# Stick-breaking attention: the norm of a head pair's second token half, in two parts in the sixth and eighth tile instead of whole in the fourth

## The chip, the cores and the metric

The kernel runs on one core of a Trainium2 chip. The metric is the device time of one execution in microseconds (us). Engines are named PE (TensorE, matmuls; PEld its weight loads), DVE (VectorE), ACT (ScalarE), POOL (GpSimd) and SP (SyncE, which starts the transfers). Each engine runs its own instruction stream in order, and the streams meet at semaphores.

## The reference, cut to what matters

The program is two transformer blocks over 1024 tokens of width 1024, in float32. The change lies in the attention of the second block. Eight heads of 64 channels are worked on; the weights of a head are

```
A[t,s] = sigmoid(z_ts) * prod_{s<j<t} (1 - sigmoid(z_tj)),  strictly causal, in log space
o_sb   = A v
y_sb   = rms_norm_2(o_sb, ones)            # over the 64 channels of each head
         * g_sb
mix    = concat(y_pool, y_sb) @ w_out
rms_norm_2(x, g) = x * rsqrt(mean(x*x) + 1e-6) * g
```

The change is in the `rms_norm_2` over each head.

## The kernel before, in words

**Layout.** Channels lie on the 128 partitions and tokens along a row, so a pair of heads fills the partitions. The four pairs are the rounds c = 0 to 3 of the loop at L2592. The 1024 queries are two halves of 512 (`H2`); a half and a block of 128 keys make a tile. `sb_pairs` (L103) lists the NP = 12 tiles p of a round: p = 0 to 3 for the first half (key blocks 3 to 0), p = 4 to 11 for the second (blocks 7 to 0). Each has both heads side by side; its width is 2x128, 2x256, 2x384 and 2x512 for the first four, the same for p = 4 to 7, then 2x512 to the end.

**A tile.** PE makes the scores (`z_pair`, L1160 and L1165). ACT makes log(1+exp(-|z|)) in three steps (`lse`, L1755, L1757, L1759). DVE adds max(z,0) (`softplus`, L2597) and splits the result into a high part (L2608) and a low part (L2610) (`split`). PE applies a triangular matrix to both (`tri_pair`, L1174, L1178) and sums them for the later tiles (`sums_pair`, L1190). DVE adds the sums of earlier tiles (`add_sums`, L2625; for the first tile of a half it clears them instead, L2618), ACT takes the exponent (`weights`, L1782) and copies the sums (`later_sums`), PE multiplies with the values (`pv_pair`, L1203).

**The order of one step p, by hand, on each engine.**
- PE: z(p+1), then at p = 4 and 6 of rounds 0 to 2 four transposes of the next round's values (`turn_v`, L1241), tri(p), sums(p), pv(p-1), then in rounds 0 to 2 `pieces(p)` (L1228): twelve matmuls of the next round's projections, four steps to a unit of weights. z(p+1) waits until add_sums(p-1) has freed its PSUM banks.
- ACT: lse(p+1), at p = 4 and 6 a copy of the turned values, weights(p), later_sums(p+1).
- DVE: split(p), at even p of rounds 0 to 2 `evac2` (L2570: one half unit of pieces, from PSUM, times the token scale), `head_mean` or `head_norm` where they are due, softplus(p+1), add_sums(p), and in round 3 at p = 3 to 9 `mix_lo(p-3)` (L2129), which waits for `mix_hi` of ACT. turn_v(0) at p = 4 waits for the evac2 of step 4, and that one for the last pieces of step 3.
- POOL: only the split of weight units (L628, L630; 128x1024 each). A unit's split starts when the matmuls of the unit before have ended, so at the end of pieces(3), pieces(7) and pieces(11).

**The norm.** Half m = 2c or 2c+1 of a round is copied out and squared by ACT (`out_half`) when its last tile is done, and the rest comes in the next round: PE takes the mean over each head (`head_mean`, L1254), DVE copies it into the tile `HM` (L2632) at p = 0 for the first half and p = 2 for the second, ACT makes a first guess of the inverse root (`head_guess`, L1797 and L1799, into `work_a`) at the end of the same step, and DVE refines and applies it (`head_norm`, four instructions on 128x512: L2639, L2641, L2643, L2645) at p = 1 and at p = 3, between split(p) and softplus(p+1). Round 0 has none of these. Round 3 has the first half of its own pair too, at p = 8 and 9; the last half comes behind the loop. The semaphore `sb_on` counts finished norms: `head_mean(m)` on DVE waits for m of them, ACT's `out_half(m)` for m-1 (m = 2c at p = 4, m = 2c+1 behind p = 11), ACT in round 3 at p = 9 for six.

Of the kernel before, what the change touches and what calls it, by code (L numbers as in the profile page):

```python
# [16 lines left out]
H2 = T // 2  # L17
EPS = 1e-6
# [90 lines left out]
def uppers_to(pairs, n):  # L109

    return sum(b > 0 for _, b, _ in pairs[:n])
# [120 lines left out]
def program(nc, x, w_glu, w_qkv, w_out, w_ff, w_ffd, w_tail, w_taild, gains, taps, rpb,  # L232
            p_t, w_in2, w_pool, w_out2, w_mlp, w_mlpd, w_plep, w_pleg, out):
    f32, f32r = mybir.dt.float32, mybir.dt.float32r
    ALU, ACT = mybir.AluOpType, mybir.ActivationFunctionType

    ctx = ExitStack()
    with ctx:
        base = 16512

        def at(name, shape, offset, dt=f32):
            return nc.alloc_sbuf_tensor_at(name, shape, dt, offset=base + offset)

        def sem(name):
            return ctx.enter_context(nc.semaphore(name))
# [17 lines left out]
        TA = at("work_a", [P, T], S0 + 8192)  # L263
# [48 lines left out]
        OB = [at(f"sb_out{c}", [P, T], QK0 + 16384 + 4096 * c) for c in range(4)]  # L312
# [9 lines left out]
        HM = at("head_mean_kept", [P, H2], R2 + 30720)  # L322
# [38 lines left out]
        s = {n: sem(n) for n in names}  # L361
# [7 lines left out]
        def sums_before(c, p):  # L369

            return c * UPS + uppers_to(PAIRS, p)

        def g(name, k=0):
            return GN[:, g_of[name] + k:g_of[name] + k + 1]
# [1632 lines left out]
        def _(dve):  # L2007
            chain = Chain(dve, s["dve_chain"])
            stt, tt, ts = dve_.scalar_tensor_tensor, dve_.tensor_tensor, dve_.tensor_scalar
# [117 lines left out]
            def mix_lo(k, src, n0, place=None):  # L2127
                dve.wait_ge(s["mix_hi"], n0 + (k if place is None else place) + 1)
                tt(INL[:, k, :], src, INH[:, k, :].bitcast(f32), ALU.subtract).then_inc(s["mix_lo"], 1)  # L2129
# [6 lines left out]
            def head_norm(i, b):  # L2136

                j, half = i // 2 % 2, slice((i % 2) * H2, (i % 2 + 1) * H2)
                t, y0, ps = (TA, TB)[j][:, half], (SQ, TC)[j][:, half], PS[:, b, :]
                dve.wait_ge(s["qk_y0"], i + 1)  # L2140
                stt(ps, ps, EPS, T2[:], ALU.add, ALU.mult).then_inc(s["qk_a"], 1)
                dve.wait_ge(s["qk_a"], i + 1)
                chain(stt(ps, ps, -3.0, y0, ALU.add, ALU.mult))
                chain.wait()
                stt(t, ps, GS[:, j:j + 1], t, ALU.mult, ALU.mult).then_inc(s["qk_scaled"], 1)
# [30 lines left out]
            weight_lo(U_QKV + 2)  # L2176
            conv(2)
            head_norm(0, 4)
            head_norm(1, 5)
            conv(1)  # L2180
            head_lo(0, 0)
# [372 lines left out]
            def evac2(j, c, half=None):  # L2554

                t, scale = (TC, TB, SQ)[j], (1.0, 1.0, DH ** -0.5)[j]
                n = U_QKV2 + 3 * c + j
                if half is None:
                    dve.wait_ge(s["unit_done"], n + 1)
                    stt(t[:], bank(2 * j), scale, RS[:], ALU.mult, ALU.mult).then_inc(s["bank_free"], 1)  # L2560
                else:
                    cols = slice(half * H2, (half + 1) * H2)
                    dve.wait_ge(s["unit_done" if half else "half_done"], n + 1 if half else 3 * (c - 1) + j + 1)
                    if j == 0 and half == 0:

                        dve.wait_ge(s["v2_tr"], 2 * c)
                    elif half == 0:

                        dve.wait_ge(s["q2_lo"], 3 * c)
                    stt(t[:, cols], PS[:, 7, :], scale, RS[:, cols], ALU.mult, ALU.mult)\  # L2570
                        .then_inc(s["bank_free" if half else "half_free"], 1)

            def q2_lo(j, c):
                cols = (slice(0, T), slice(0, H2), slice(H2, T))[j]
                if j == 1 and c:
                    dve.wait_ge(s["half_free"], 3 * c)
                else:
                    dve.wait_ge(s["bank_free"], U_QKV2 + 3 * c + min(j, 1) + 2)
                dve.wait_ge(s["q2_hi"], 3 * c + j + 1)
                tt((KL, QL, QL)[j][:, cols], (TB, SQ, SQ)[j][:, cols], (KH, QH, QH)[j][:, cols].bitcast(f32),  # L2580
                   ALU.subtract).then_inc(s["q2_lo"], 1)
# [10 lines left out]
            for c in range(4):  # L2592
                def softplus(p):
                    half, b, lo = PAIRS[p]
                    e, zb = EX[p % 2][:, :, lo:], 2 * (p % 2)
                    dve.wait_ge(s["sb_lse"], NP * c + p + 1)
                    chain(stt(e, PS[:, zb:zb + 2, lo:], 0.0, e, ALU.max, ALU.add))  # L2597

                def split(p):
                    half, b, lo = PAIRS[p]  # L2600
                    e, N = EX[p % 2][:, :, lo:], NP * c + p
                    if N >= 2:

                        n = p - 1
                        dve.wait_ge(s["sb_up"], c * UPS + uppers_to(PAIRS, n) if n > 0 else c * UPS)
                        dve.wait_ge(s["sb_cum"], N - 1)
                    chain.wait()
                    dve_.tensor_copy(SPH[p % 2][:, :, lo:], e).then_inc(s["sb_hi"], 1)  # L2608
                    dve.wait_ge(s["sb_hi"], N + 1)
                    tt(SPL[p % 2][:, :, lo:], e, SPH[p % 2][:, :, lo:].bitcast(f32), ALU.subtract)\  # L2610
                        .then_inc(s["sb_sp"], 1)

                def add_sums(p):
                    half, b, lo = PAIRS[p]
                    N, zb = NP * c + p, 2 * (p % 2)
                    if b == 4 * half + 3:

                        dve_.memset(TS[:, :, 0:H2 - P], 0.0).then_inc(s["sb_tz"], 1)  # L2618
                        return
                    dve.wait_ge(s["sb_cum"], N + 1)  # L2620
                    dve.wait_ge(s["sb_ts"], sums_before(c, p))
                    if N >= 2:

                        dve.wait_ge(s["sb_pv"], N - 1)
                    tt(AW[p % 2][:, :, lo:], PS[:, zb:zb + 2, lo:], TS[:, :, lo:], ALU.add).then_inc(s["sb_add"], 1)  # L2625

                def head_mean(m):

                    dve.wait_ge(s["sb_osum"], m + 1)
                    if m:  # L2630
                        dve.wait_ge(s["sb_on"], m)
                    dve_.tensor_copy(HM[:], PS[:, 7, :]).then_inc(s["sb_om"], 1)  # L2632

                def head_norm(m):

                    cols = slice((m % 2) * H2, (m % 2 + 1) * H2)
                    ps, y0, o = HM[:], TA[:, cols], OB[m // 2][:, cols]
                    dve.wait_ge(s["sb_o0"], m + 1)
                    chain(stt(ps, ps, EPS, y0, ALU.add, ALU.mult))  # L2639
                    chain.wait()  # L2640
                    chain(stt(ps, ps, -0.5, y0, ALU.mult, ALU.mult))  # L2641
                    chain.wait()
                    chain(stt(y0, ps, 1.5, y0, ALU.add, ALU.mult))  # L2643
                    chain.wait()
                    stt(o, o, g("g_sb", m // 2), y0, ALU.mult, ALU.mult).then_inc(s["sb_on"], 1)  # L2645

                softplus(0)
                for p in range(NP):
                    split(p)
                    if c < 3 and p % 2 == 0 and p:  # L2650
                        evac2((p // 2 - 1) // 2, c + 1, (p // 2 - 1) % 2)
                    if p == 0 and c:
                        head_mean(2 * c - 2)
                    elif p == 2 and c:
                        head_mean(2 * c - 1)
                    elif c == 3 and p == 8:
                        head_mean(6)

                    if p == 1 and c:
                        head_norm(2 * c - 2)  # L2660
                        q2_lo(2, c)
                    elif p == 3 and c:
                        head_norm(2 * c - 1)
                    elif c == 3 and p == 9:
                        head_norm(6)
                    if p + 1 < NP:
                        softplus(p + 1)
                    elif c < 3:
                        q2_lo(0, c + 1)
                        q2_lo(1, c + 1)  # L2670
                    add_sums(p)
                    if c == 3 and 3 <= p < 10:
                        mix_lo(p - 3, MIX2[p - 3], 8)
                if c < 3:
                    evac2(2, c + 1, 1)
            head_mean(7)
            head_norm(7)

            mix_lo(7, OB[3][:], 8)
            dve.wait_ge(s["mix_lo"], 16)  # L2680
# [205 lines left out]
```

## Time and profile before

| what | value |
|---|---|
| time, median of 3 runs (lowest to highest) | 2570.45 us (2567.76 to 2574.14) |
| the profiled execution: its own time | 2575.64 us |
| its span in the trace | 2573.9 us |
| mean granted TensorE clock over the span | 0.951 of full |
| busy: PE, DVE, ACT, POOL | 2354.7, 1612.1, 1112.5, 1197.5 us |
| the four rounds of the attention loop | from 1292.7 to 1659.5 us of the span |

All times in the rows below are from the start of the profiled execution's span. The duration of a row runs to the modelled end of the instruction; on PE and DVE the next one begins a little before that end, so distances from start to start are used where instructions follow each other closely. A bracket at the end of a row is the idle time of that engine before the instruction, and what ended it.

### The profile page before, as it was taken

What the parts mean: (1) busy time and instruction counts of PE and PEld (TensorE: products, weight loads), DVE (VectorE), ACT (ScalarE), POOL (GpSimd) and SP (SyncE); (2) the same over time, 40 slices, a digit from 0 to 9 for tenths busy, and PEclk for the clock granted to TensorE, in tenths of its full rate; (3) what the DMA queues carried; (4) which work ended last, traced back from release to release, by engine and by line L of the source; (5) the groups of instructions that cost most, each with busy time, mean ns of one, the idle gap of its engine ahead of it and who ended that gap; (6) DMA issues with size and microseconds to landing.
All of it is one profiled execution on the core that took longest, in us unless ns stands there. A gap on an engine that the chain in (4) does not pass through costs nothing.

```text
span 2573.9 us, 28774 instructions
## 1 busy us (share of the span) xinstructions
PE 2354.7 (91%) x10304; PEld 1819.0 (71%) x10304; DVE 1612.1 (63%) x1852; ACT 1112.5 (43%) x1779; POOL 1197.5 (47%) x845
## 2 busy tenths in 40 slices
PE   8988886989999999999988987797899999999978
PEld 6866554768888887887755554484688878888757
DVE  7888863396565667466557566547766656444656
ACT  4255545244444443223055656505566652222331
POOL 1000000358877878776311110042677767777553
PEclk9989987989999999999989998798999999999989
DMA  3211100413434439963100000112356577966112
GB/s 129 58 32 32 33 17 1 172 41 123 160 111 179 164 115 351 379 234 113 39 17 25 17 9 1 78 69 82 147 237 267 231 296 303 365 258 256 50 33 90
DMA packets 88156, 342.10 MB, mean 133 GB/s; under 512 B 22288, under 2 KB 22288, under 8 KB 75088
## 3 DMA queue, kind: packets, MB, share of 16 engines
q1 hardware_dynamic: 87360, 335.86, 34.9%
q10 hardware_dynamic: 656, 4.41, 0.4%
q8 instruction: 83, 1.36, 0.2%
q14 instruction: 57, 0.47, 0.1%
HBM read 224.16 MB, written 116.27 MB: 132 GB/s over the span
## 4 chain that ended last, share of the span: by engine, by line
PE 70%; DVE 11%; issue 9%; ACT 6%; POOL 3%; DMA 1%; SPq 0%; DVEq 0%; POOLq 0%; ACTq 0%
PE ps L990 45%; PE ps L755 16%; PE ps L1228 2%; POOL turn_weights L666 1%; DVE operand L2296 1%; PE ps L1203 1%; PE ps L1160 1%; DVE sb_weights L2625 1%; ACT sb_e L1757 1%; DVE sb_softplus_lo L2610 1%; ACT sb_e L1755 1%; DMA weight_raw<-w_out 1%; ACT sb_e L1759 1%; DVE conv_out L2099 1%; DVE operand L2298 1%
## 5 line engine op out<-in xcount | busy, mean ns | idle before, releaser
L990 PE MATMUL ps<-operand,turn_weights 128*128 128x512 f32 x3192 | 743.6, 395 | 23.3 <-DVE operand L2296 11.6
L990 PEld LDWEIGHTS ps<-operand,turn_weights 128*128 128x128 f32 x3192 | 605.0, 190 | 161.3 <-issue 23.1
L666 POOL TENSOR_TENSOR turn_weights<-turn_raw,turn_weights 128x512 fp32r<-128x512 f32 (+1 forms) x330 | 443.5, 1354 | 238.3 <-ACT turn_weights L1348 237.4
L628 POOL TENSOR_TENSOR weight_hi<-weight_raw,zero_col 128x1024 fp32r<-128x1024 f32 (+1 forms) x42 | 83.8, 1995 | 944.8 <-PE ps L755 688.1
L990 PE MATMUL ps<-hidden_operand,turn_weights 128*128 128x512 f32 x2268 | 518.4, 390 | 3.5 <-issue 1.9
L990 PEld LDWEIGHTS ps<-hidden_operand,turn_weights 128*128 128x128 f32 x2268 | 426.2, 188 | 95.6 <-issue 5.4
L2478 DVE TENSOR_TENSOR branch_out<-ps,branch_out 128x1024 f32<-128x1024 f32 x172 | 210.5, 1224 | 203.1 <-PE ps L990 202.1
L1348 ACT ACTIVATE turn_weights<-turn_raw 128x512 fp32r<-128x512 f32 (+1 forms) x330 | 205.1, 623 | 266.0 <-PE ps L990 257.1
L755 PE MATMUL ps<-input_lo,weight_hi 128*128 128x512 f32 x816 | 261.6, 403 | 17.6 <-DVE gate_lo L2802 15.8
L755 PE MATMUL ps<-input_hi,weight_hi 128*128 128x512 f32 x688 | 229.2, 415 | 27.9 <-DVE input_lo L2057 10.3
L755 PE MATMUL ps<-input_hi,weight_lo 128*128 128x512 f32 x688 | 217.6, 398 | 0.0
L755 PEld LDWEIGHTS ps<-input_lo,weight_hi 128*128 128x128 f32 x816 | 158.4, 195 | 55.6 <-ACT input_lo L1348 12.7
L666 POOL TENSOR_TENSOR turn_weights<-weight_sums,turn_weights 128x512 fp32r<-128x512 f32 (+1 forms) x132 | 174.6, 1322 | 12.9 <-ACT turn_weights L1348 2.6
L755 PEld LDWEIGHTS ps<-input_hi,weight_hi 128*128 128x128 f32 x688 | 129.3, 195 | 66.1 <-issue 32.8
L1348 ACT ACTIVATE turn_weights<-weight_sums 128x512 fp32r<-128x512 f32 (+1 forms) x132 | 82.4, 626 | 208.4 <-POOL weight_sums L670 207.5
L2099 DVE SCALAR_TENSOR_TENSOR conv_out<-glu_padded,taps_sb,conv_out 128x1024 f32<-128x1024 f32 x120 | 153.8, 1281 | 2.9
L755 PEld LDWEIGHTS ps<-input_hi,weight_lo 128*128 128x128 f32 x688 | 132.8, 193 | 29.1
L670 POOL TENSOR_TENSOR weight_sums<-weight_sums,turn_raw 128x512 f32<-128x512 f32 (+1 forms) x66 | 90.2, 1366 | 80.3 <-PE ps L990 79.7
L630 POOL TENSOR_TENSOR weight_lo<-weight_raw,weight_hi 128x1024 fp32r<-128x1024 f32 (+1 forms) x42 | 107.7, 2565 | 3.3
L2597 DVE SCALAR_TENSOR_TENSOR sb_e<-ps,sb_e 128x1024 f32<-128x1024 f32 (+3 forms) x48 | 45.9, 955 | 98.1 <-ACT sb_e L1759 98.0
L670 POOL TENSOR_TENSOR weight_sums<-turn_raw 128x512 f32<-128x512 f32 (+1 forms) x66 | 94.8, 1437 | 15.3 <-PE ps L990 13.8
L2360 DVE TENSOR_TENSOR ps<-ps,gate_act 128x512 f32<-128x512 f32 x44 | 30.8, 699 | 102.3 <-PE ps L990 102.2
(314 smaller groups left out, 3445.3 us busy)
## 6 DMA issues: line engine op xcount, KB each, us to landing
hidden_operand<-hidden_kept SPq DMA_DIRECT2D x91, 1024.0 KB, 7.9
hidden_kept<-hidden_parts SPq DMA_DIRECT2D x54, 1024.0 KB, 8.8
hidden_kept<-hidden_parts SPq DMA_DIRECT2D x27, 1536.0 KB, 5.9
turn_raw<-w_ff SPq DMA_DIRECT2D x40, 512.0 KB, 4.1
turn_raw<-w_mlp SPq DMA_DIRECT2D x32, 512.0 KB, 4.3
turn_raw<-w_mlpd SPq DMA_DIRECT2D x32, 512.0 KB, 4.4
turn_raw<-w_ffd SPq DMA_DIRECT2D x20, 512.0 KB, 4.6
weight_raw<-w_out SPq DMA_DIRECT2D x16, 512.0 KB, 3.5
```

The lines of the kernel that those rows point to most:

```text
L628: pool_.tensor_tensor(WH[:, slot, 0:width], raw, ZERO[:].to_broadcast([P, width]), ALU.add).then_inc(s["w_hi"], 1)
L630: pool_.tensor_tensor(WL[:, slot, 0:width], raw, WH[:, slot, 0:width].bitcast(f32), ALU.subtract).then_inc(s["w_split"], 1)
L666: pool_.tensor_tensor(place(p, 1), place(p, 1, WT) if raw is None else raw, bits(place(p, 0)), ALU.subtract).then_inc(s["st_lo"], 1)
L670: pool_.tensor_tensor(out, x, y, op).then_inc(s["st_sum"], 1)
L755: last = mm(PS[:, b + 2 * c + h, :], w[:, slot, k * n + P * c:k * n + P * (c + 1)], a[:, k, h * H2:(h + 1) * H2], start=(k == first and st ...
L990: ins = mm(PS[:, b, :], weights(p, w, k), tokens(p, a, k), start=(FRESH[p] and k == 0 and step == 0), stop=(k == n - 1 and step == 2), ski ...
L1228: last = mm(PS[:, 7, :], w[:, v % 2, k * P:(k + 1) * P], a[:, k, half * H2:(half + 1) * H2], start=(k == 0 and step == 0), stop=(k == KD - ...
L1348: copy = lambda out, in_, scale=1.0: act_.activation(out, in_, ACT.Copy, scale=scale)
L2099: ins = stt(Y[:, c, :], src, TP[:, c, t:t + 1], Y[:, c, :], ALU.mult, ALU.add)
L2360: ins = tt(out, PS[:, 3 * (t % 2) + ROLE[p], :], y, op)
L2478: ins = tt(here(X if last else MM), PS[:, b:b + 2, :], here(MM), ALU.add)
L2597: chain(stt(e, PS[:, zb:zb + 2, lo:], 0.0, e, ALU.max, ALU.add))
```

## The change: what it does

`head_norm` is cut in two: `head_root` holds its first two instructions (and the wait for ACT's guess), `head_scaled` the other two (and the count of `sb_on`). For the first half of a pair, and for half 6 and half 7, the two parts stand where `head_norm` stood. For the second half of a pair (m = 2c-1, in rounds 1, 2 and 3), `head_root` goes to step p = 5 and `head_scaled` to step p = 7; step p = 3 has neither. PE, ACT, POOL and SP are not touched.

```diff
-                def head_norm(m):
-
+                def head_root(m):
+
+                    y0 = TA[:, (m % 2) * H2:(m % 2 + 1) * H2]
+                    dve.wait_ge(s["sb_o0"], m + 1)
+                    chain(stt(HM[:], HM[:], EPS, y0, ALU.add, ALU.mult))
+                    chain.wait()
+                    chain(stt(HM[:], HM[:], -0.5, y0, ALU.mult, ALU.mult))
+
+                def head_scaled(m):
                     cols = slice((m % 2) * H2, (m % 2 + 1) * H2)
-                    ps, y0, o = HM[:], TA[:, cols], OB[m // 2][:, cols]
-                    dve.wait_ge(s["sb_o0"], m + 1)
-                    chain(stt(ps, ps, EPS, y0, ALU.add, ALU.mult))
+                    y0, o = TA[:, cols], OB[m // 2][:, cols]
                     chain.wait()
-                    chain(stt(ps, ps, -0.5, y0, ALU.mult, ALU.mult))
-                    chain.wait()
-                    chain(stt(y0, ps, 1.5, y0, ALU.add, ALU.mult))
+                    chain(stt(y0, HM[:], 1.5, y0, ALU.add, ALU.mult))
                     chain.wait()
                     stt(o, o, g("g_sb", m // 2), y0, ALU.mult, ALU.mult).then_inc(s["sb_on"], 1)
...
                     if p == 1 and c:
-                        head_norm(2 * c - 2)
+                        head_root(2 * c - 2)
+                        head_scaled(2 * c - 2)
                         q2_lo(2, c)
-                    elif p == 3 and c:
-                        head_norm(2 * c - 1)
+                    elif p == 5 and c:
+                        head_root(2 * c - 1)
+                    elif p == 7 and c:
+                        head_scaled(2 * c - 1)
                     elif c == 3 and p == 9:
-                        head_norm(6)
+                        head_root(6)
+                        head_scaled(6)
```

## Rows read from the trace of the kernel before

**Rows 1.** Windows, rounds 0 to 3 of the attention loop.
```profile
core 0: us, PE busy (x) PEld busy (x) DVE busy (x) ACT busy (x) POOL busy (x), PEclk, DMA share, GB/s
1292.70:1379.90 87.20, 80.78 (x376) 53.65 (x376) 47.39 (x57) 49.90 (x64) 11.13 (x5) 0.94 0.04 13
1379.90:1472.30 92.40, 81.75 (x382) 53.33 (x380) 57.88 (x67) 54.34 (x71) 13.82 (x7) 0.94 0.05 18
1472.30:1564.70 92.40, 81.83 (x382) 53.19 (x380) 57.86 (x67) 54.33 (x71) 13.91 (x7) 0.94 0.04 12
1564.70:1659.50 94.80, 62.02 (x233) 33.93 (x231) 58.96 (x71) 59.14 (x76) 2.79 (x2) 0.75 0.00 1
```

**Rows 2.** Windows, from z(5) to z(6) on PE, in rounds 0, 1, 2.
```profile
1322.00:1328.50 6.50, 6.28 (x37) 4.44 (x36) 3.08 (x5) 4.13 (x8) 4.28 (x2) 1.00 0.15 28
...
1406.90:1420.90 14.00, 9.90 (x36) 6.78 (x36) 7.27 (x7) 5.49 (x9) 4.08 (x2) 0.63 0.11 37
...
1499.40:1513.20 13.80, 9.72 (x36) 6.65 (x36) 7.22 (x7) 5.45 (x9) 4.03 (x2) 0.63 0.12 38
```

**Rows 3.** Timeline of PE, round 1, z(5) and turn_v(0): start, us, engine, line.
```profile
1406.91 0.39 PE L1160 MATMUL ps<-q_hi,k_hi 64*128 64x256 f32 x2 [0.26 <-DVE sb_weights L2625]
...
1411.99 1.11 PE L1241 MATMUL ps<-identity,work_c 128*128 128x128 f32 x4 [4.09 <-DVE work_c L2570]
```

**Rows 4.** Timeline of DVE, round 1, steps 3 to 5.
```profile
1402.46 0.69 DVE L2639 SCALAR_TENSOR_TENSOR head_mean_kept<-head_mean_kept,work_a 128x512 f32<-128x512 f32 x1 [1.02 <-ACT work_a L1799]
...
1405.31 0.42 DVE L2597 SCALAR_TENSOR_TENSOR sb_e<-ps,sb_e 128x256 f32<-128x256 f32 x1
1405.64 1.22 DVE L2625 TENSOR_TENSOR sb_weights<-ps,sb_later_sums 128x1024 f32<-128x1024 f32 x1
1406.78 2.01 DVE L2608 CAST sb_softplus_hi<-sb_e 128x256 fp32r<-128x256 f32 x1
1408.82 2.52 DVE L2610 TENSOR_TENSOR sb_softplus_lo<-sb_e,sb_softplus_hi 128x256 fp32r<-128x256 f32 x1
...
1424.71 0.96 DVE L2597 SCALAR_TENSOR_TENSOR sb_e<-ps,sb_e 128x768 f32<-128x768 f32 x1 [10.36 <-ACT sb_e L1759]
```

**Rows 5.** Timeline of POOL, round 1.
```profile
1406.74 1.89 POOL L628 TENSOR_TENSOR weight_hi<-weight_raw,zero_col 128x1024 fp32r<-128x1024 f32 x1 [23.97 <-PE ps L1228]
1408.71 2.35 POOL L630 TENSOR_TENSOR weight_lo<-weight_raw,weight_hi 128x1024 fp32r<-128x1024 f32 x1
1441.30 2.13 POOL L628 TENSOR_TENSOR weight_hi<-weight_raw,zero_col 128x1024 fp32r<-128x1024 f32 x1 [30.24 <-PE ps L1228]
```

**Rows 6.** Timeline of ACT, round 1, the last step of lse(4).
```profile
1403.18 0.42 ACT L1759 ACTIVATE sb_e<-sb_e 128x256 f32<-128x256 f32 x1
```

**Rows 7.** Timeline of DVE, round 0: L2608 of split(4), evac2, softplus(6), softplus(8).
```profile
1319.92 0.28 DVE L2608 CAST sb_softplus_hi<-sb_e 128x256 fp32r<-128x256 f32 x1
...
1322.11 0.69 DVE L2570 SCALAR_TENSOR_TENSOR work_c<-ps,token_scale 128x512 f32<-128x512 f32 x1 [1.45 <-PE ps L1228]
...
1332.30 0.96 DVE L2597 SCALAR_TENSOR_TENSOR sb_e<-ps,sb_e 128x768 f32<-128x768 f32 x1 [4.77 <-ACT sb_e L1759]
...
1346.28 1.22 DVE L2597 SCALAR_TENSOR_TENSOR sb_e<-ps,sb_e 128x1024 f32<-128x1024 f32 x1 [3.81 <-ACT sb_e L1759]
```

**Rows 8.** Timeline of DVE, round 3: softplus(4), softplus(6), softplus(8).
```profile
1590.74 0.42 DVE L2597 SCALAR_TENSOR_TENSOR sb_e<-ps,sb_e 128x256 f32<-128x256 f32 x1
...
1604.49 0.96 DVE L2597 SCALAR_TENSOR_TENSOR sb_e<-ps,sb_e 128x768 f32<-128x768 f32 x1 [0.16 <-ACT sb_e L1759]
...
1619.85 1.23 DVE L2597 SCALAR_TENSOR_TENSOR sb_e<-ps,sb_e 128x1024 f32<-128x1024 f32 x1
```

**Rows 9.** Timeline of ACT, round 3: end of lse(4), start of lse(7).
```profile
1588.62 0.42 ACT L1759 ACTIVATE sb_e<-sb_e 128x256 f32<-128x256 f32 x1
...
1608.88 1.02 ACT L1755 ACTIVATE sb_e<-ps 128x1024 f32<-128x1024 f32 x1 [0.75 <-PE ps L1165]
```

**Rows 10.** Timeline of PE, round 3: z(5), and the low part of tri(7).
```profile
1592.35 0.58 PE L1160 MATMUL ps<-q_hi,k_hi 64*128 64x256 f32 x2 [3.90 <-DVE sb_weights L2625]
...
1619.90 1.22 PE L1178 MATMUL ps<-sb_softplus_lo,minus_tri_r 128*128 128x512 f32 x2
```

More of the change, by code:

```diff
@@ L2676, in _ @@
             head_mean(7)
-            head_norm(7)
+            head_root(7)
+            head_scaled(7)
             mix_lo(7, OB[3][:], 8)
```

## The prediction, made before the changed kernel ran

> **What bounds the kernel now.** I began with the page: PE is busy 91% of the span and carries 70% of the chain that ended last, so a change on DVE can only pay where PE waits for DVE. The norm lives in the attention loop, so I cut the span into its four rounds with the windows view [rows 1]. Rounds 0, 1 and 2 do the same matmuls, but round 0 takes 87.2 us (with the start of the loop in it) and the others 92.4 each, at a clock of 0.94. Round 3 is another regime: PE is busy only 62.0 of 94.8 us and has 0.75 of its clock; DVE (59.0 busy) and ACT (59.1) pass the work to and fro there. I then cut each round at the scores and found one step that differs: from z(5) to z(6) it is 6.5 us in round 0, which has no norm, and 14.0 and 13.8 us in rounds 1 and 2 [rows 2]. PE is busy 6.28 us in the one, 9.90 and 9.72 in the others for the same work, with the clock at 1.00 against 0.63. That step is what the change is about.
>
> **Why it is long.** The PE timeline of round 1 shows two waits in that step: 0.26 us before z(5), for add_sums(3), and 4.09 us before turn_v(0), for the evac2 of DVE [rows 3]. The DVE timeline says why evac2 is late [rows 4]. DVE ended split(3) at about 1401.4, idled 1.02 us for ACT's guess, and spent 2.85 us (1402.46 to 1405.31) on the four norm instructions; softplus(4) and add_sums(3) followed, and split(4) began at 1406.78. By then POOL had begun the two passes of a weight split, at 1406.74 and 1408.71, ending at 1411.06 [rows 5]. The cast of split(4) took 2.01 us where the same cast takes 0.28 in round 0 [rows 7], and L2610 took 2.52; each ended a little after a pass of POOL. So DVE stood behind POOL for about 4 us, and evac2, which could have run at 1406.8, ran at 1411.3. PE, idle for those 4.09 us, then fell to the lower of its two levels, 1.2 GHz, and did the rest of the step at it: four matmuls of L1241 took 1.11 us. The chain of waits walks through the same instructions in this order: guess, norm, softplus, split, evac2, turn_v.
>
> **The change part by part.**
>
> *The norm leaves step 3, rounds 1 and 2.* Without it softplus(4) starts when ACT has ended lse(4), at 1403.60 [rows 6], say 1403.7 instead of 1405.31: 1.6 us earlier. (The guess on ACT stays where it was, ahead of lse(4), so the 1.02 us of idle time turns into part of the wait for lse(4).) add_sums(3), 0.33 us behind softplus(4), then starts at 1404.0 and split(4) 1.14 later, at 1405.2; undisturbed its cast needs 0.28 us [rows 7], L2610 I take at 0.4, and it is done by 1405.9. POOL starts when pieces(3) end, and nothing moves those: 1406.74, 0.8 us later. DVE is idle when pieces(3) end, evac2 runs at once, as in round 0 where it waited 1.45 us for PE and took 0.69 beside the same POOL passes [rows 7], and reads one operand from PSUM. z(5) no longer waits (0.26 us), and turn_v(0) finds its data a tenth of a microsecond before or after z(5) ends. That is the state of round 0, so I take round 0's 6.5 us for the step. Gains: 0.26 + 14.0 - 6.5 = 7.8 us in round 1 and 0.26 + 13.8 - 6.5 = 7.6 us in round 2, together **15.3 us**. Some 4.1 of each is the wait, some 3.4 the clock. The lower bound for each is the waits alone, 4.35; the upper is the 7.8, since the PE work itself stays.
>
> *head_root enters step 5, rounds 1 and 2.* Two instructions, 0.72 us from start to start, 1.4 us together. They stand between split(5) and softplus(6), and the latter waits for ACT anyhow: 4.77 us in round 0's form of the step [rows 7], 10.36 in round 1 now [rows 4]. Cost zero; with that cover gone, 1.4. They read two SBUF tiles, as L2610 does, but POOL has ended about a microsecond before them; a meeting would cost up to 2.0 us (a cast's stall), still under 4.77.
>
> *head_scaled enters step 7, rounds 1 and 2.* 1.4 us ahead of softplus(8), which waits 3.81 us for ACT [rows 7]; POOL's next split begins only at 1441.30, when pieces(7) end, and DVE has the two done before them [rows 5]. Cost zero; uncovered 1.4. Later `sb_on` holds nobody: its next readers are ACT's out_half behind p = 11 and DVE's own head_mean of the next round. No DMA and no other queue is moved past: SP's x_back waits for the last pv and its loads for the next stage for all eight norms.
>
> *Round 3.* Here nothing hides DVE, and no POOL split runs in these steps (POOL is busy 2.79 us in the round, at its start [rows 1]). Softplus(4) starts at 1590.74 [rows 8], lse(4) ended at 1589.04 [rows 9]; so step 3 gains 1.6 us, and as z(5) waited 3.90 us for it [rows 10], the whole round moves up by that. At step 5 softplus(6) had only 0.16 us of idle time before it [rows 8], so head_root pushes it by 1.4 - 0.16 = 1.2, less what the wait for lse(6) had rounded off: 1.1. ACT's weights(5) and mix_hi(2) and DVE's mix_lo(2) go with it, but lse(7) had waited 0.75 us for z(7) [rows 9], so about 0.3 of it reaches softplus(7). At step 7 softplus(8) had no idle time at all [rows 8]: head_scaled pushes it by 1.4, and with the 0.3 that is 1.7; add_sums(7) was held until 1621.1 by tri(7) on PE [rows 10], 0.2 after DVE could have gone on (softplus(8) and 1.14), so 1.5 passes. Sum for round 3: -1.6 + 1.5 = **-0.1 us**. Bounds: -1.6 if both parts are hidden, +1.2 if both come whole (2.8).
>
> The clock of round 3 is the loose end. It goes between the two levels now (0.75 as a mean), and with new starting points the stretches fall elsewhere. The step z(5) to z(6) of rounds 1 and 2 shows a price: 3.4 us for a step that is done at 1.2 GHz instead of 2.4. I allow one such stretch more or less, 3 us either way, and put none in the sum. The Trainium skill, in TensorE: Matmul & The Clock Gate, Part 1, says that the point at which the clock changes varies from run to run with the phase of a free-running counter; by that round 3 would come out differently from run to run, with the same mean as now. No row here can show it.
>
> **The sum.** -7.8 - 7.6 - 0.1 = -15.5 us. Against the profiled execution's own 2575.64 that gives 2560.1; that execution lies 5.2 us above the median of the three runs, and as nothing in the sum depends on where those 5.2 arose, I take the difference over to the median: 2570.45 - 15.5 = **2554.9 us**. Behind the loop the rest is PE's and moves up as a whole.
>
> **The rivals.**
>
> *A, the forecast:* 2554.9 us. For it: round 0, the same step without a norm, in the same trace. Its own range is 2550 to 2560.
>
> *B, the wait goes but the clock isn't given back.* If z(5), turn_v and what follows have some gap that round 0 hasn't, PE works at 1.2 GHz there still. Gain 2 x 4.35 + 0.1 = 8.8 us: 2561.6. Against it: PE in round 0 was without work for 0.22 of the 6.50 us too, and kept 1.00 [rows 2].
>
> *C, the meeting with POOL stays, so the change doesn't do what it's there for.* Split(4) is late for a second reason than the norm. The Trainium skill, in SBUF — State Buffer, under "SBUF: two separate sides", says that VectorE and GpSimd share a port pair, that whichever starts first holds it for its whole instruction and that the other is blocked until then. The trace agrees with it (2.01 against 0.28 us). By that rule 0.8 us of margin decide all or nothing. In this kernel that would mean: if split(4) starts after 1406.7, it is stopped as before, rounds 1 and 2 gain 0.26 at most, and the time is 2570. Against it: lse(4) ended at 1403.60 and nothing but softplus and add_sums stands between.
>
> *D, slower: round 3 loses its clock.* In round 3 both parts stand on a DVE with no idle time, PE waits longer for it in steps 5 to 8, and could stay at 1.2 GHz for the whole round. PE's 62.0 us at 0.75 are 46.5 us of work at full clock and 93.0 at half: 31.0 us more, an upper bound as PE idles a third of the round [rows 1]. With all of it, 2570.45 - 15.5 + 31.0 = 2586 us. It decides the sign once more than half of that bound is real. Against it: PE waits there for DVE already (3.90 us at z(5) [rows 10]), and the steps in question grow by 1.1 and 1.4.
>
> **How the numbers follow.** A 0.86, B 0.06, C 0.05, D 0.03. A measurement of this kernel tells 0.3%, 7.7 us, from no change. All of A lies beyond that bound (below 2562.7); B is at 2561.6, just beyond it, and I give it half to faster and half to same. Faster: 0.86 + 0.03 = 0.89. Same: 0.03 + 0.05 = 0.08. Slower: 0.03. The range runs from 2549.5 (A with one half-clock stretch less, and 2.5 us of the runs' own scatter) to 2562 (one stretch more and that scatter, with B in it); it leaves out C, D and about one tenth of A's tails.
>
> **What the profile would show.** Right: in rounds 1 and 2 the cast of split(4) takes 0.3 us and starts before POOL's L628; turn_v(0) waits under 0.3 us; z(5) to z(6) is 6.5 us at clock 1.00; the rounds are 84.6 and 84.8 us long; L2639 stands in front of a wait of softplus(6) of over 3 us. In round 3 z(5) waits some 2.3 us instead of 3.9, softplus(6) and softplus(8) have no idle time before them, and the round keeps 94 to 95 us. Wrong: a cast of 2 us in step 4, a clock under 0.9 from z(5) to z(6), or a round 3 over 98 us.

## The result, and the profile after

The changed kernel takes 2560.20 us as the median of 8 runs (2555.22 to 2563.13), the kernel before in the same sessions 2572.38 (2567.76 to 2575.75, 8 runs). The ratio is 0.9949, with a 95% interval of 0.9940 to 0.9958; as a share of 2572.38 us that is 13.1 us less (10.8 to 15.4), while the two medians lie 12.2 us apart. The forecast was 2554.9, 15.5 us less, in a range of 2549.5 to 2562.

The profiled execution's span fell from 2573.9 to 2558.5 us. Its page, part 1 (busy time, share of the span, instructions) and the clock over 40 slices:

```profile
span 2558.5 us, 28774 instructions
...
PE 2343.9 (92%) x10304; PEld 1813.3 (71%) x10304; DVE 1605.0 (63%) x1852; ACT 1111.5 (43%) x1779; POOL 1197.5 (47%) x845
...
PEclk9989997989999999999989997898899999999989
```

The same instructions ran. PE lost 10.8 us of busy time and DVE 7.1: both had taken longer for the same work. The windows view of the four rounds, columns as in [rows 1]:

```profile
1291.80:1379.00 87.20, 80.88 (x376) 53.62 (x376) 47.39 (x57) 49.87 (x64) 11.08 (x5) 0.94 0.04 13
1379.00:1465.10 86.10, 79.59 (x384) 51.86 (x382) 54.17 (x67) 54.00 (x71) 13.94 (x7) 0.98 0.06 19
1465.10:1549.60 84.50, 77.98 (x382) 50.95 (x380) 54.18 (x67) 54.01 (x71) 13.88 (x7) 1.00 0.04 13
1549.60:1643.40 93.80, 61.91 (x233) 34.64 (x231) 58.59 (x71) 59.01 (x76) 2.82 (x2) 0.75 0.00 1
```

Round 0 is untouched, round 2 has lost 7.9 us, round 1 only 6.3, round 3 1.0. The same view from z(5) to z(6) in rounds 1 and 2, beside the 14.00 and 13.80 of [rows 2], and then step 8 (z(9) to z(10)) in the two rounds:

```profile
1405.70:1412.20 6.50, 6.28 (x39) 4.46 (x38) 4.03 (x7) 4.12 (x8) 4.27 (x2) 1.00 0.11 27
1491.70:1498.20 6.50, 6.29 (x37) 4.45 (x36) 3.98 (x7) 4.12 (x8) 4.29 (x2) 1.00 0.14 23
1432.40:1442.80 10.40, 8.62 (x31) 5.06 (x30) 8.09 (x7) 6.93 (x7) 5.36 (x2) 0.84 0.19 52
1518.40:1527.40 9.00, 7.21 (x33) 4.22 (x32) 7.83 (x7) 6.51 (x7) 5.39 (x2) 1.00 0.00 0
```

The step in question is round 0's, to the hundredth, with the clock at its upper level. The third row is something new: step 8 of round 1 took 9.0 us before (window of the kernel before below) and takes 10.4 now, at 0.84 of the clock.

```profile
1441.10:1450.10 9.00, 7.21 (x33) 4.21 (x32) 7.83 (x7) 6.51 (x7) 5.38 (x2) 1.00 0.19 58
```

The DVE timeline of round 1 after the change answers to [rows 4] (in the changed kernel the four norm instructions are L2638, L2640, L2646, L2648):

```profile
1402.76 0.42 DVE L2597 SCALAR_TENSOR_TENSOR sb_e<-ps,sb_e 128x256 f32<-128x256 f32 x1 [2.19 <-ACT sb_e L1759]
1403.10 1.22 DVE L2625 TENSOR_TENSOR sb_weights<-ps,sb_later_sums 128x1024 f32<-128x1024 f32 x1
1404.23 0.28 DVE L2608 CAST sb_softplus_hi<-sb_e 128x256 fp32r<-128x256 f32 x1
1404.55 0.43 DVE L2610 TENSOR_TENSOR sb_softplus_lo<-sb_e,sb_softplus_hi 128x256 fp32r<-128x256 f32 x1
1405.81 0.69 DVE L2570 SCALAR_TENSOR_TENSOR work_c<-ps,token_scale 128x512 f32<-128x512 f32 x1 [0.83 <-PE ps L1228]
...
1411.13 0.69 DVE L2638 SCALAR_TENSOR_TENSOR head_mean_kept<-head_mean_kept,work_a 128x512 f32<-128x512 f32 x1
1411.85 0.69 DVE L2640 SCALAR_TENSOR_TENSOR head_mean_kept<-head_mean_kept,work_a 128x512 f32<-128x512 f32 x1
```

Beside it POOL and PE, answering to [rows 5] and [rows 3]:

```profile
1405.85 1.90 POOL L628 TENSOR_TENSOR weight_hi<-weight_raw,zero_col 128x1024 fp32r<-128x1024 f32 x1 [23.96 <-PE ps L1228]
```

```profile
1405.70 0.39 PE L1160 MATMUL ps<-q_hi,k_hi 64*128 64x256 f32 x2
1406.56 0.66 PE L1241 MATMUL ps<-identity,work_c 128*128 128x128 f32 x4
```

Split(4) is done 0.9 us before POOL starts. The cast takes 0.28 us instead of 2.01, L2610 0.43 instead of 2.52, evac2 waits for PE and not the other way round, and neither z(5) nor turn_v(0) waits. L1241 takes 0.66 us instead of 1.11: the upper clock.

**Step lengths.** From here on I use one measure for every trace: the distance between the starts of z(p) and z(p+1) on PE (the first L1160 of each), and the length of the loop from the first z(0) to the last pv (L1203). It is worked out from timelines like those above, and leaves out what differs from execution to execution elsewhere: the first z(0) comes at 1292.72 us in the trace before, at 1291.83 in this one, and between 1285.6 and 1294.5 in the traces below, although all these kernels are the same up to there; what follows the loop took 915.4 us before and 913.2 to 916.8 in the others.

| | before | changed |
|---|---|---|
| round 1, z(4) to z(6) | 19.92 | 12.08 |
| round 2, z(4) to z(6) | 19.79 | 12.06 |
| round 1, z(9) to z(10) | 8.94 | 10.44 |
| round 3, z(0) to the last pv | 93.76 | 92.74 |
| loop | 365.76 | 350.56 |

The loop is 15.20 us shorter: 7.84 + 7.73 - 1.50 + 1.02 makes 15.09 of it, and the rest is spread over other steps.

### The profile page after: what moved, and what is told of

Its sections match the earlier page's. It is cut to its first block, busy times and chain, and to the rows that moved or that the text cites. A ratio compares the mean times of both kernels' runs of the same rounds, so it can differ in the third digit from the quotient of the medians.

```text
span 2558.5 us, 28774 instructions
## 1 busy us (share of the span) xinstructions
PE 2343.9 (92%) x10304; PEld 1813.3 (71%) x10304; DVE 1605.0 (63%) x1852; ACT 1111.5 (43%) x1779; POOL 1197.5 (47%) x845
## 4 chain that ended last, share of the span: by engine, by line
PE 69%; DVE 11%; issue 9%; ACT 6%; POOL 3%; DMA 1%; SPq 0%; DVEq 0%; POOLq 0%; ACTq 0%
PE ps L990 45%; PE ps L755 16%; PE ps L1228 3%; DVE operand L2296 1%; POOL turn_weights L666 1%; ACT sb_e L1757 1%; PE ps L1160 1%; ACT sb_e L1755 1%; DVE sb_weights L2625 1%; DMA weight_raw<-w_out 1%; DVE sb_softplus_lo L2610 1%; ACT sb_e L1759 1%; DVE residual L2806 1%; DVE operand L2298 1%; PE ps L1203 1%
## 5 line engine op out<-in xcount | busy, mean ns | idle before, releaser
L628 POOL TENSOR_TENSOR weight_hi<-weight_raw,zero_col 128x1024 fp32r<-128x1024 f32 (+1 forms) x42 | 83.6, 1991 | 927.1 <-PE ps L755 684.6
L670 POOL TENSOR_TENSOR weight_sums<-turn_raw 128x512 f32<-128x512 f32 (+1 forms) x66 | 94.9, 1437 | 15.4 <-PE ps L990 13.8
```

The source lines that it names most:

```text
L628: pool_.tensor_tensor(WH[:, slot, 0:width], raw, ZERO[:].to_broadcast([P, width]), ALU.add).then_inc(s["w_hi"], 1)
L670: pool_.tensor_tensor(out, x, y, op).then_inc(s["st_sum"], 1)
```

## The experiments

Nine more runs were made, in three sessions, each beside the kernel before on the same chip. Their medians scatter by 2 or 3 us, so a difference between two of them of that size says little by itself; the loop in the trace is the sharper measure, and both are given.

**The changed kernel again.**

> The changed kernel once more, unaltered, for a second trace and more times on the chip that the next three run on. The first trace moved by -15.4 us where the medians moved by 12 to 13. It also showed one thing that the forecast had not: in round 1, step 8, PE dropped to 1.2 GHz for a moment after its 1.8 us wait for L2610 and lost 1.5 us. Theory 'phase': such drops fall here or there from execution to execution; this trace then differs from the first by one or two of them (1.5 to 3 us of span), while z(5) to z(6) is 6.5 us in rounds 1 and 2 again; the time is 11 to 15 us below the kernel before. Rival 'fixed': the drop at step 8 of round 1 is a steady cost of the change and is there again, with the same 1.5 us.

Measured: 2559.64 us, ratio 0.9943 (0.9929 to 0.9956); loop 350.61 us, against 350.56 in the first trace. z(4) to z(6) is 12.08 us in both rounds. The drop at step 8 of round 1 is there again, 10.50 us. "Phase" falls for the loop and "fixed" stands: between these two traces the loop and its rounds repeat (round 3 is 92.74 and 92.73 us), and the 1.2 us between their spans arose outside it. The row of PE in step 8 of round 1, this kernel:

```profile
1434.51 1.22 PE L1178 MATMUL ps<-sb_softplus_lo,minus_tri_r 128*128 128x512 f32 x2 [1.78 <-DVE sb_softplus_lo L2610]
```

Two matmuls take 1.22 us where they take 0.74 at the same place in round 2, after a wait of 1.76 us.

**Rounds 1 and 2 alone.** Round 3 has its norm at step 3 again.

```diff
-                    elif p == 5 and c:
+                    elif p == 3 and c == 3:
+                        head_root(5)
+                        head_scaled(5)
+                    elif p == 5 and c in (1, 2):
                         head_root(2 * c - 1)
-                    elif p == 7 and c:
+                    elif p == 7 and c in (1, 2):
                         head_scaled(2 * c - 1)
```

> The change in rounds 1 and 2 alone; round 3 has the whole norm at step 3 as before. Theory 'meeting' (the gain is the removal of DVE's meeting with POOL in step 4, and PE's clock after it, in rounds 1 and 2; round 3 gives back what it gains): within 1.5 us of the changed kernel, round 3 at 94 to 95 us with a wait of 3.9 us before z(5). Rival 'round 3 takes part' (the 1.6 us gained at step 3 of round 3 are kept): 1.5 to 3 us slower than the changed kernel.

Measured: 2559.99 us, ratio 0.9939 (0.9925 to 0.9952); loop 350.18 us, 0.4 less than the changed kernel. The wait before z(5) of round 3 is 3.90 us as before. So the gain lies in rounds 1 and 2, and moving the norm in round 3 is worth nothing. One part of the expectation failed: round 3 was to take 94 to 95 us and took 92.35. It has the instructions and the order of the kernel before, whose round 3 took 93.76, so 1.4 us of difference in round 3 need no change in it; the changed kernel's 92.74 is 0.4 us more than this.

**The norm in place, POOL held back.** This run takes away the meeting and leaves the norm where it was. On the kernel before, with POOL's loop over the units written out:

```diff
-            splits(U_POOL + 2, U_PLEP - U_POOL - 2)
+            for n in range(U_PLEP - U_POOL - 2):
+                u = U_POOL + 2 + n
+                for c in (1, 2):
+                    for p, j in ((4, 5),):
+                        if u == U_QKV2 + 3 * c + j:
+                            pool.wait_ge(s["sb_sp"], NP * c + p + 1)
+                split(u, n % 2, 16 * (n // 2) + 8 * (U_POOL + 2) + 16)
```

> The kernel before, norm whole at step 3, but in rounds 1 and 2 POOL holds its weight split back until DVE has finished split(4). Theory 'meeting': the cast of split(4) takes 0.3 us and L2610 0.4, evac2 runs at about 0.7 us behind POOL's old start, turn_v waits 0.5 us instead of 4.1, the clock stays at 1.00, z(5) to z(6) is about 7 us; 13 to 14 us less than the kernel before, nearly the whole gain with the norm where it was. Rival 'load' (PE waits for the 2.85 us of norm that DVE does in step 3): the wait of turn_v stays at 2.5 us or more and the gain is under 4 us.

Measured: 2558.90 us, ratio 0.9937 (0.9924 to 0.9951); loop 349.80 us, 0.8 less than the changed kernel. DVE, POOL and PE of round 1 (in this kernel the split is L2614 and L2616, evac2 L2576, turn_v L1247):

```profile
1404.14 0.28 DVE L2614 CAST sb_softplus_hi<-sb_e 128x256 fp32r<-128x256 f32 x1
1404.46 0.42 DVE L2616 TENSOR_TENSOR sb_softplus_lo<-sb_e,sb_softplus_hi 128x256 fp32r<-128x256 f32 x1
1404.80 0.68 DVE L2576 SCALAR_TENSOR_TENSOR work_c<-ps,token_scale 128x512 f32<-128x512 f32 x1
```

```profile
1404.96 1.89 POOL L628 TENSOR_TENSOR weight_hi<-weight_raw,zero_col 128x1024 fp32r<-128x1024 f32 x1 [24.76 <-DVE sb_softplus_lo L2616]
```

```profile
1404.28 0.39 PE L1166 MATMUL ps<-q_hi,k_hi 64*128 64x256 f32 x2 [0.27 <-DVE sb_weights L2631]
1405.54 0.66 PE L1247 MATMUL ps<-identity,work_c 128*128 128x128 f32 x4 [0.27 <-DVE work_c L2576]
```

A delay of POOL by 0.8 us (its idle time is 24.76 us instead of 23.97) does what moving 2.85 us of DVE work does. turn_v waits 0.27 us with the four norm instructions still ahead of it; z(5) to z(6) is 6.68 and 6.69 us. "Load" is out: nearly all that the norm cost PE came from pushing split(4) behind POOL's start. What is left is 0.5 us a round: z(4) to z(6) is 12.60 and 12.61 us, against 12.08 and 12.06. The loop is 16.0 us shorter than before, more than the 13 to 14 expected: 14.5 of it in step 4 of the two rounds, 1.5 in round 3 (92.28 us), which is unaltered here. Against the changed kernel the 0.5 us a round is more than made up, as this kernel has no drop at step 8 (9.00 us in round 1).

**Putting 1.4 us back.** head_root goes into step 3, behind add_sums(3).

```diff
-                    elif p == 5 and c:
-                        head_root(2 * c - 1)
...
                     add_sums(p)
+                    if p == 3 and c:
+                        head_root(2 * c - 1)
```

> The changed kernel with head_root of the second half not at step 5 but in step 3, between add_sums(3) and split(4), in rounds 1 to 3: 1.4 us of DVE work put back ahead of split(4). In the trace of the changed kernel split(4) began 1.62 us before POOL. Theory 'meeting': the cast starts 0.25 us before POOL, L2610 behind it is stopped until POOL's first pass ends (1.9 us instead of 0.4 for it) and turn_v waits 2 to 2.5 us; z(5) to z(6) 9 us or more (up to 12 if the clock falls), and the time is 4 to 9 us above the changed kernel, less about 1 us gained in round 3, where this place has idle time. Rival 'load': 1.4 us more on DVE against a slack of 0.8 us: turn_v waits 0.6 us, and the time is within 1.5 us of the changed kernel.

Measured: 2565.90 us, ratio 0.9969 (0.9957 to 0.9981); loop 357.12 us, 6.6 more than the changed kernel (4.9 and 2.0 in step 4 of rounds 1 and 2, less 0.6 in round 3; the drop at step 8 moved from round 1 to round 2, which all but cancels). DVE in round 1, and turn_v(0) of PE in rounds 1 and 2:

```profile
1402.31 0.30 DVE L2608 CAST sb_softplus_hi<-sb_e 128x256 fp32r<-128x256 f32 x1
1402.64 2.00 DVE L2610 TENSOR_TENSOR sb_softplus_lo<-sb_e,sb_softplus_hi 128x256 fp32r<-128x256 f32 x1
```

```profile
1405.29 1.12 PE L1241 MATMUL ps<-identity,work_c 128*128 128x128 f32 x4 [2.05 <-DVE work_c L2570]
...
1494.89 0.66 PE L1241 MATMUL ps<-identity,work_c 128*128 128x128 f32 x4 [2.06 <-DVE work_c L2570]
```

The cast slipped in 0.1 us before POOL, whose L628 began at 1402.40; L2610 did not and stood until the pass was over: 2.00 us. The wait of 2.05 us is the "meeting" forecast. And the windows view from z(5) to z(6) gives the clock's price by itself:

```profile
1402.25:1413.67 11.42, 9.37 (x37) 6.37 (x37) 5.38 (x7) 4.45 (x8) 4.38 (x2) 0.70 0.16 46
1491.84:1500.32 8.48, 6.42 (x38) 4.45 (x38) 5.39 (x7) 4.35 (x8) 4.40 (x2) 1.00 0.21 62
```

The same wait, within a hundredth of a microsecond, once with a fall of the clock behind it and once without: 11.42 against 8.48 us. The fall costs 2.94 us.

**Putting 0.7 us back.** Only the first instruction of head_root stands behind add_sums(3), the second stays at step 5; a second argument of `head_root` picks the instruction (its code is left out here).

```diff
-                        head_root(2 * c - 1)
+                        head_root(2 * c - 1, 1)
...
                     add_sums(p)
+                    if p == 3 and c:
+                        head_root(2 * c - 1, 0)
```

> As the run with head_root in step 3, but with only its first instruction there (0.72 us between add_sums(3) and split(4)); the second stays at step 5. That run showed the 2.05 us wait of turn_v in both rounds. Theory 'meeting': it is a threshold. Split(4) now ends at 1.62 - 0.72 - 0.75 = 0.15 us before POOL starts, so no pass of POOL is met, L2610 takes 0.43 us, turn_v waits nothing, z(5) to z(6) is 6.5 us in rounds 1 and 2, and the time is within 1.5 us of the changed kernel. Rival 'load': half the work, half the loss: turn_v waits 1.0 us and z(5) to z(6) is 7.5 us.

Measured: 2559.77 us, ratio 0.9939 (0.9923 to 0.9954); loop 350.04 us. DVE, POOL and turn_v(0) of PE in round 1:

```profile
1408.02 0.43 DVE L2610 TENSOR_TENSOR sb_softplus_lo<-sb_e,sb_softplus_hi 128x256 fp32r<-128x256 f32 x1
```

```profile
1408.52 1.89 POOL L628 TENSOR_TENSOR weight_hi<-weight_raw,zero_col 128x1024 fp32r<-128x1024 f32 x1 [23.95 <-PE ps L1228]
```

```profile
1409.22 0.66 PE L1241 MATMUL ps<-identity,work_c 128*128 128x128 f32 x4
```

L2610 ends 0.07 us before POOL starts, turn_v waits nothing, z(5) to z(6) is 6.49 and 6.50 us. One instruction costs nothing, two cost 6.6 us: a threshold, not a rate.

**POOL held back at steps 4 and 8.** The changed kernel, with waits as in the third run, for the splits behind pieces(3) (until split(4)) and behind pieces(7) (until split(8)), in rounds 0 to 2.

```diff
...
+                for c in range(3):
+                    for p, j in ((4, 5), (8, 6)):
+                        if u == U_QKV2 + 3 * c + j:
+                            pool.wait_ge(s["sb_sp"], NP * c + p + 1)
...
```

> The changed kernel, and POOL holds its splits back until split(4) and split(8) are done, in rounds 0 to 2. Step 4 has no meeting left; step 8 has one in every round (L2610 takes 2.80 us instead of 1.23, PE waits 1.78 us), and in round 1 of all traces of the changed kernel PE's clock fell behind it, which cost 1.5 us more. Theory: L2610 of split(8) takes 1.23 us, PE's wait there goes to 0.2 us or less, z(9) to z(10) falls from 9.0 to about 7.5 us in each of the three rounds and from 10.4 to 7.5 in round 1: 4.5 + 1.5 = 6 us below the changed kernel. Rival: POOL's passes, moved behind split(8), meet split(9), or PE waits for ACT instead: under 2 us.

Measured: 2556.68 us, ratio 0.9933 (0.9920 to 0.9947); loop 347.02 us, 3.5 less than the changed kernel, where 6 were expected. The step itself did as forecast:

```profile
1432.17 1.22 DVE L2616 TENSOR_TENSOR sb_softplus_lo<-sb_e,sb_softplus_hi 128x1024 fp32r<-128x1024 f32 x1
```

```profile
1433.45 0.73 PE L1184 MATMUL ps<-sb_softplus_lo,minus_tri_r 128*128 128x512 f32 x2 [0.21 <-DVE sb_softplus_lo L2616]
...
1440.94 0.73 PE L1184 MATMUL ps<-sb_softplus_lo,minus_tri_r 128*128 128x512 f32 x2 [0.23 <-DVE sb_softplus_lo L2616]
```

z(9) to z(10) is 7.47 us in all three rounds, and round 1's drop is gone. But z(10) to z(11) went from 6.90 to 7.49, and from there to the next z(0) from 15.36 to 15.60. The reason, as I read the traces: step 9 has a wait for DVE too (the last row), and takes 7.5 us like step 8, the pace of the circle of PE, ACT and DVE. In the changed kernel the long step 8 had given ACT a lead and the next step was the shorter for it: in round 1 ACT idled 2.02 us for PE before lse(10) there, and starts it without a wait here. So the meeting at step 8 is worth 0.7 us a round and not 1.5; with the 1.5 of the drop that makes 3.6.

**Round 3's norms into DVE's idle time.**

```diff
-                    elif p == 5 and c:
+                    elif p == 5 and c in (1, 2):
                         head_root(2 * c - 1)
-                    elif p == 7 and c:
+                    elif p == 7 and c in (1, 2):
                         head_scaled(2 * c - 1)
-                    elif c == 3 and p == 9:
-                        head_root(6)
-                        head_scaled(6)
...
                     add_sums(p)
+                    if c == 3 and p == 4:
+                        head_root(5)
+                        head_scaled(5)
+                    elif c == 3 and p == 9:
+                        head_root(6)
+                        head_scaled(6)
```

> The changed kernel, and in round 3 both norms that stand between a split and a softplus go into DVE's idle time ahead of mix_lo: that of half 5 whole behind add_sums(4) (4.4 us idle there), that of half 6 behind add_sums(9) (3.0 us idle). Theory (in round 3 DVE between split and softplus is on the path, DVE ahead of mix_lo is not): the 1.2 us that the two parts gave back and the 2.8 us of half 6 go, round 3 takes 89.5 to 90.5 us, 3.5 to 4.5 us below the changed kernel. Rival 'ACT sets the pace of round 3': mix_hi and the weights come no earlier, under 1.5 us.

Measured: 2552.33 us, ratio 0.9919 (0.9906 to 0.9933); loop 346.70 us, 3.9 less than the changed kernel; round 3 is 88.8 us (1543.55 to 1632.31) against 92.7. DVE, from the last norm instruction of half 5 to softplus(6):

```profile
1576.85 0.75 DVE L2648 SCALAR_TENSOR_TENSOR sb_out<-sb_out,gains_sb,work_a 128x512 f32<-128x512 f32 x1
1579.19 1.23 DVE L2129 TENSOR_TENSOR input_lo<-pool_u,input_hi 128x1024 fp32r<-128x1024 f32 x1 [1.59 <-ACT input_hi L1348]
1580.34 0.42 DVE L2608 CAST sb_softplus_hi<-sb_e 128x512 fp32r<-128x512 f32 x1
1580.79 0.69 DVE L2610 TENSOR_TENSOR sb_softplus_lo<-sb_e,sb_softplus_hi 128x512 fp32r<-128x512 f32 x1
1581.64 0.96 DVE L2597 SCALAR_TENSOR_TENSOR sb_e<-ps,sb_e 128x768 f32<-128x768 f32 x1 [0.16 <-ACT sb_e L1759]
```

DVE still idles 1.59 us behind the norm, and softplus(6) has its 0.16 us of idle time back. The 3.9 us are in the range that was expected, the 88.8 us for the round are below it (89.5 to 90.5). The median is 7.3 us under that of the changed kernel's second run. The loop shows 3.9 of it; in this trace z(0) of round 0 comes 5 to 6 us earlier and the part behind the loop is 3 us shorter, with nothing changed in either, so I take 3.9 for the change.

**Both.**

> The last two together. They lie in different rounds and should add: 9 to 11 us below the changed kernel, 0.990 of the kernel before or less. If the one undoes the other through PE's clock, the sum is short by 1.5 to 3 us.

Measured: 2552.20 us, ratio 0.9919 (0.9905 to 0.9932); loop 343.18 us, 7.4 less than the changed kernel. 3.5 and 3.9 add up; the sum is short of the 9 to 11 expected because the POOL part was, and not by an interaction. This has the shortest loop of all. By whole runs it can't be told from the run before.

**The norm whole in step 5.**

```diff
                     elif p == 5 and c:
                         head_root(2 * c - 1)
-                    elif p == 7 and c:
                         head_scaled(2 * c - 1)
```

> The norm of the second half whole in step 5 (2.85 us between split(5) and softplus(6)) in rounds 1 to 3; step 7 has none. Theory: what counts is that it has left step 3, not that it is cut in two. In rounds 1 and 2 DVE waits 4.8 us for ACT there, so 2.85 us fit: z(5) to z(6) 6.5 us, z(6) to z(8) as in the changed kernel. In round 3 the whole 2.85 us stand on the path at step 5 instead of 1.4 at 5 and 1.4 at 7, less the 0.75 us that lse(7) waited: round 3 within 1 us of the changed kernel. Time within 1.5 us of it. Rival 'two parts are needed': 2.85 us delay softplus(6) in rounds 1 and 2 as well; their z(7) to z(9) grow by over 1 us each and the time is 2 to 4 us above the changed kernel.

Measured: 2559.28 us, ratio 0.9942 (0.9928 to 0.9955); loop 352.11 us. In rounds 1 and 2 every step is as in the changed kernel; softplus(6) still waits 1.93 us for ACT:

```profile
1412.37 0.96 DVE L2597 SCALAR_TENSOR_TENSOR sb_e<-ps,sb_e 128x768 f32<-128x768 f32 x1 [1.93 <-ACT sb_e L1759]
```

In round 3, z(6) to z(7) is 8.99 us instead of 7.49, and the round 94.2 instead of 92.7, more than the 1 us I had allowed. But 1.0 of these 1.4 us lies in step 11, from z(11) to the last pv: 14.63 us instead of 13.60, the length it has in the kernel before too (14.67), with PE at its lower clock in pv(10). From z(0) to z(11) the whole norm costs 0.4 us more than the two parts. So cutting the norm in two is worth nothing in rounds 1 and 2 and 0.4 us in round 3; whether the step-11 stretch belongs to it as well is open.

## Why the prediction was right, point by point

*The norm leaves step 3, rounds 1 and 2* (forecast 7.8 and 7.6): 7.84 and 7.73. Right in every link that can be read: softplus(4) came 1.6 us earlier, the cast and L2610 of split(4) took 0.28 and 0.43 us, turn_v waited nothing, the clock stayed up, and round 0 was the right model. The third run shows the cause by itself: without the meeting, the norm in step 3 costs 0.5 us a round and not 7.8. The fourth and fifth show the margin of rival C at work: I had put it at 0.8 us, the trace has 0.9; 0.7 us of work fit in it and 1.4 do not. So C and B did not happen, but C was as near as its sentence said. By the rule of the Trainium skill (SBUF — State Buffer, "SBUF: two separate sides"), who starts first holds the pair to the end of his instruction: the trace agrees in the fourth run, where the cast that began 0.1 us before POOL took 0.30 us, and L2610 0.2 us behind POOL's start took 2.00. On POOL's side it is less clear: its pass began 0.2 us before that cast ended and took only 0.06 us longer than elsewhere.

*head_root and head_scaled in rounds 1 and 2* (0): 0. Softplus(6) waits for ACT still, and so does softplus(8) in step 7 (2.43 us of idle time before it in the changed kernel, 3.83 before). The last run puts the whole norm in step 5 and pays nothing there.

*Round 3* (-0.1): -1.02 against the trace of the kernel before. The gain at step 3 was 1.66 us (1.6; z(5) waits 2.22 us, where 2.3 were forecast), the loss at softplus(6) 1.08 (1.1) and at softplus(8) 1.31 (1.4). Of the first loss 0.59 us reached softplus(7), not 0.3. The forecast saw that softplus(6) delays weights(5) and mix_hi(2), but took z(7) on PE as unmoved; z(7) needs the banks that add_sums(5) frees, and that stands behind softplus(6). z(7) of round 3, before and after:

```profile
1606.58 0.79 PE L1160 MATMUL ps<-q_hi,k_hi 64*128 64x512 f32 x2
```

```profile
1590.44 0.80 PE L1160 MATMUL ps<-q_hi,k_hi 64*128 64x512 f32 x2 [0.51 <-DVE sb_weights L2625]
```

Up to softplus(11) the terms leave the round 0.05 us longer, and the forecast's -0.1 was near. The rest lies in step 11, where add_sums(11) waited 0.81 us for PE where it had waited 1.88. pv(10) on PE and add_sums(11) on DVE, before, changed, and in the second run (round 3 as before):

```profile
1652.74 1.98 PE L1203 MATMUL ps<-sb_weights,v_tokens 128*64 128x512 f32 x4
...
1656.11 1.22 DVE L2625 TENSOR_TENSOR sb_weights<-ps,sb_later_sums 128x1024 f32<-128x1024 f32 x1 [1.88 <-PE ps L1178]
```

```profile
1637.47 1.08 PE L1203 MATMUL ps<-sb_weights,v_tokens 128*64 128x512 f32 x4
...
1640.02 1.22 DVE L2625 TENSOR_TENSOR sb_weights<-ps,sb_later_sums 128x1024 f32<-128x1024 f32 x1 [0.81 <-PE ps L1178]
```

```profile
1638.12 1.08 PE L1203 MATMUL ps<-sb_weights,v_tokens 128*64 128x512 f32 x4
...
1640.49 1.23 DVE L2625 TENSOR_TENSOR sb_weights<-ps,sb_later_sums 128x1024 f32<-128x1024 f32 x1 [0.83 <-PE ps L1178]
```

PE is at its lower clock in the first pair and at its upper one in the others. That is one stretch of the clock less, which the forecast had allowed for and put at zero. It is not the work of moving the norm within the round: the second and third run have the norm at step 3 and gain it too (rounds of 92.35 and 92.28 us). Measured against the second run, the move costs 0.4 us. Rival D, round 3 losing its clock, did not happen: 0.75 as before.

*What was missing*: step 8 of round 1, 1.50 us. The sum had the clock's uncertainty in round 3 alone. Step 8 has a wait of 1.78 us for L2610, which meets POOL too, in every round and in both kernels; before the change none of the three was followed by a fall of the clock, after it that of round 1 was. So the forecast's 84.6 us for round 1 was missed (86.1), and its 84.8 for round 2 met (84.5). The drop is in each of the six traces whose rounds 1 and 2 run step 4 without a wait and without holding POOL back at step 8. Where z(5) and turn_v wait 0.27 us each (third run) it isn't there; with the waits of 2.05 us (fourth run) it comes in round 2 instead, 10.52 us. So it goes with the timing of the kernel rather than with chance, as far as one execution of each can tell. Why round 1 and not the others is open.

*The sum* (-15.5): the loop gave -15.20. Part of that closeness is luck: the +1.50 of step 8 and the -1.07 of step 11, both from the clock, were not in the sum and largely cancel; the 15.3 us of rounds 1 and 2 are the part that was worked out. Ahead of it the trace is 0.9 us shorter and behind it 0.7 longer, neither with a cause in the change, and so the span moved by -15.4. The times moved by 13.1 us (10.8 to 15.4) and, in the next session, by 14.7 (11.3 to 18.3), both from the ratios. Forecast for the median 2554.9, measured 2560.2: of the 5.3 us, 1.9 are the kernel before, whose median over eight runs is 2572.4 and not 2570.45; the rest is the step-8 drop and scatter that I can't divide further.

## What to carry to other kernels

When an instruction takes several times its usual length, look at what another engine does in that time before counting the work ahead of it: the cost of DVE and POOL meeting is a threshold of where they stand in time. It can be removed from either side, and here a wait on POOL, which had 24 us to spare, did as much as moving DVE's work. A stage of the same kernel that runs the step without the extra work is a good model for its length after the change; here it gave the two large terms within 0.2 us. And in a loop where two engines pass work to and fro, work belongs in an idle gap: in round 3 the two norms took 3.9 us off the loop when they went from between split and softplus to ahead of mix_lo. Last, before a small difference in such a stage is put down to a change, look at it in a run that leaves the stage alone: round 3 with the same instructions took 93.76 us in one kernel and 92.35 in another, more than the 0.4 us that the move cost there.

## What the runs showed of the hardware

- The same wait of PE (2.05 and 2.06 us, same work before and after) was followed by the lower clock in one round and not in the other, and the difference was 2.94 us. Waits of 4.09 and 4.08 us were followed by it in both rounds; waits of 1.76 to 1.79 us at step 8 were in round 1 of six traces (10.42 to 10.50 us for the step) and not in rounds 0 and 2 of the same traces (8.90 to 8.98).
- A cast that started 0.1 us before POOL's pass was not slowed (0.30 us), POOL's pass behind it took 1.95 instead of 1.89 us; the subtraction that followed the cast took 2.00 us instead of 0.43. What reads one of its two tiles from PSUM was not slowed beside POOL in the loop: evac2 takes 0.68 or 0.69 us there and elsewhere, softplus of 128x1024 at step 8 1.22 or 1.23.
- Removing a stall of 1.6 us at step 8 shortened the step by 1.5 us and the round by 0.7.
